# Splitting the key/value product of a streaming hybrid block into two K halves, and moving the last head's outputs

## What is computed

```
h = rmsnorm(x); p = h @ w_in            # 2816 columns, split into
qa, ka, va = 8 query heads, 2 key and 2 value heads of 64     (windowed attention)
qb, fb, ib, gb = 4 heads of 128 each                          (HGRN2 gated recurrence)
ya = attention(rope(rmsnorm(qa)), rope(rmsnorm(ka)), va)      # own 64-chunk and the one before, sinks
yb = rmsnorm(o_intra + o_inter) * silu(gb)                    # chunkwise recurrence
x = x + concat(ya, yb) @ w_out
x = x + (silu(h2 @ w_gate) * (h2 @ w_up)) @ w_down            # h2 = rmsnorm(x)
```

## Time and profile before

| what | value |
|---|---|
| median of 3 runs | 2125.22 us (2124.48 to 2125.67) |
| the profiled execution | 2124.75 us, of which 2123.0 us are the span that the trace shows |
| TensorE busy in the span | 2097.5 us (99%), 11128 matmuls |
| VectorE busy | 1305.7 us (62%) |
| ScalarE busy | 825.3 us (39%) |
| moved by transfers | 395.77 MB, mean 186 GB/s |

### The profile page before, as it was taken

How to read it: one execution, slowest core, us unless ns; L and a number is a source line. 1 busy time by engine, 2 the same in 40 slices (tenths; PEclk the granted TensorE clock), 3 DMA queues, 4 the chain that set the end, 5 groups by cost and what they waited for, 6 DMA issues and landing times.

```text
span 2123.0 us, 28527 instructions
## 1 busy us (share of the span) xinstructions
PE 2097.5 (99%) x11128; PEld 1770.7 (83%) x11128; DVE 1305.7 (62%) x1998; ACT 825.3 (39%) x1454; POOL 99.2 (5%) x108
## 2 busy tenths in 40 slices
PE   7999999999999998999999999999999999999999
PEld 7889889889988787888888888888888888888887
DVE  4674654554467875777777677777777754444332
ACT  4783573573464333433233243333333322222221
POOL 2101100100100000000000000000000000000000
PEclk9999999999999999999999999999999999999999
DMA  7857735844546675444445345545445575555532
GB/s 264 282 201 278 296 140 194 303 160 155 218 159 238 217 252 218 142 142 140 149 145 184 105 140 173 193 152 190 144 149 164 183 250 189 201 173 173 178 134 90
DMA packets 194262, 395.77 MB, mean 186 GB/s; under 512 B 11408, under 2 KB 117136, under 8 KB 172752
## 3 DMA queue, kind: packets, MB, share of 16 engines
q1 hardware_dynamic: 187616, 363.27, 49.7%
q0 software_dynamic: 6512, 30.67, 3.9%
HBM read 268.60 MB, written 125.30 MB: 186 GB/s over the span
## 4 chain that ended last, share of the span: by engine, by line
PE 60%; DVE 0%; DVEq 0%; ACT 0%; issue 0%
PE b_bank_A L373 4%; PE b_bank_A L371 4%; PE b_bank_A L372 4%; PE b_bank_C L373 4%; PE b_bank_B L373 4%; PE b_bank_C L371 4%; PE b_bank_B L371 4%; PE b_bank_B L372 4%; PE b_bank_C L372 4%; PE b_hx_bank L1985 3%; PE b_hx_bank L1984 3%; PE b_hx_bank L1986 3%; PE b_bank_D L371 2%; PE b_bank_D L373 2%; PE b_bank_D L372 2%; PE b_hx_bank L1929 1%
## 5 line engine op out<-in xcount | busy, mean ns | idle before, releaser
L1870 ACT ACTIVATE b_s_hi<-b_s_stage 128x1408 fp32r<-128x1408 f32 x56 | 77.5, 1383 | 299.9 <-PE b_hx_bank L1986 143.4
L371 PE MATMUL a_pj<-a_w_hi,a_hT_hi 128*128 128x256 f32 x640 | 185.0, 289 | 1.5 <-DVE a_hT_lo L1256 1.5
L373 PE MATMUL a_pj<-a_w_hi,a_hT_lo 128*128 128x256 f32 x640 | 180.6, 282 | 0.0
L372 PE MATMUL a_pj<-a_w_lo,a_hT_hi 128*128 128x256 f32 x640 | 180.6, 282 | 0.0
L371 PE MATMUL a_pj<-a_hT_hi,a_w_hi 128*128 128x512 f32 x384 | 154.6, 403 | 0.0
L373 PE MATMUL a_pj<-a_hT_hi,a_w_lo 128*128 128x512 f32 x384 | 150.2, 391 | 0.0
L372 PE MATMUL a_pj<-a_hT_lo,a_w_hi 128*128 128x512 f32 x384 | 150.0, 391 | 0.0
L371 PE MATMUL b_bank_A<-b_h_hi_B,b_w_hi 128*128 128x512 f32 x352 | 137.9, 392 | 0.0
L373 PE MATMUL b_bank_A<-b_h_hi_B,b_w_lo 128*128 128x512 f32 x352 | 137.4, 390 | 0.0
L372 PE MATMUL b_bank_A<-b_h_lo_B,b_w_hi 128*128 128x512 f32 x352 | 137.4, 390 | 0.0
L371 PE MATMUL b_bank_B<-b_h_hi_T,b_w_hi 128*128 128x512 f32 x352 | 137.3, 390 | 0.0
(11 more groups left out here) (309 smaller groups left out, 5080.0 us busy)
## 6 DMA issues: line engine op xcount, KB each, us to landing
b_gu_stage<-w_gu SPq DMA_DIRECT2D x44, 1024.0 KB, 5.3
b_s_stage<-a_sums SPq DMA_DIRECT2D x56, 704.0 KB, 4.1
a_w_hi<-w_parts SPq DMA_DIRECT2D x30, 1024.0 KB, 4.8
a_w_lo<-w_parts SPq DMA_DIRECT2D x30, 1024.0 KB, 7.2
a_sums<-b_a SPq DMA_DIRECT2D x88, 256.0 KB, 4.8
a_sums<-b_gate SPq DMA_DIRECT2D x66, 256.0 KB, 3.6
b_hx<-hc POOLq DMA_DIRECT2D x12, 1024.0 KB, 5.1
b_w_blocks<-w_dn SPq DMA_DIRECT2D x11, 1024.0 KB, 4.9
```

Of the source, the lines that this page charges most:

```text
L371: pe.matmul(out, stationary[0](k), moving[0](k), start=(k == 0 and not adds), stop=False, skip_group_check=adds)
L372: pe.matmul(out, stationary[0](k), moving[1](k), start=False, stop=False, skip_group_check=adds)
L373: last = pe.matmul(out, stationary[1](k), moving[0](k), start=False, stop=(k == ends), skip_group_check=adds)
L1870: act.activation(f.s_hi[n % 2][:], f.s_stage[n % 2][:], ACT.Copy).then_inc(f.s_hi_ready, 1)
```

## The change

For blocks 1 to 3 the KV chunk is no longer computed one token tile at a time. At its first group TensorE does the lower four K tiles of all four token tiles, then the upper four of tiles 0 and 1. The upper four of tiles 2 and 3 follow as groups 2 and 3, each after ScalarE has copied out the tile that shares its bank. Tiles 0 and 2 share bank 0, tiles 1 and 3 bank 1: the two results lie side by side in a bank (`kv_out`). The number of matmuls is the same. The transpose of the eighth K tile now comes after the first 12 matmuls, as before, but the product that needs it comes after 36 others.

In `LAST_HEAD`, `yt` of head 2 moves from (KV, 2) to (KV, 3), `o`, `on1` and `on2` of head 3 move from (KV, 2) to (QA0, 0), and `yt` of head 3 moves from (QA0, 0) to (QA0, 2). `ds` and `att` keep their places, (KV, 0) and (KV, 1).

```diff
-LAST_HEAD = {("KV", 0): (("on2", 2), ("ds", 3, 0), ("ds", 3, 1),), ("KV", 1): (("att", 3),), ("KV", 2): (("o", 3), ("yt", 2), ("on1", 3), ("on2", 3),), ("QA0", 0): (("yt", 3),)}
+LAST_HEAD = {("KV", 0): (("on2", 2), ("ds", 3, 0), ("ds", 3, 1),), ("KV", 1): (("att", 3),), ("KV", 3): (("yt", 2),), ("QA0", 0): (("o", 3), ("on1", 3), ("on2", 3),), ("QA0", 2): (("yt", 3),)}

+    def kv_out(b, t):
+        first = WC * (t // 2) if b > 0 else 0
+        return pj[t % 2][:, first:first + WC]
...
                     elif name == "KV":
+                        ps = kv_out(b, g)
...
-                    if (b > 0 or at >= 2) and not second_half:
+                    if b > 0 and name == "KV":
+                        if g > 1:
+                            pe.wait_ge(kv_ready.sem, kv_ready.upto(b, g - 1))
+                    elif (b > 0 or at >= 2) and not second_half:
...
-                        last = three_passes(pe, pj[at % 2][:, 0:WC], still, moving, range(KT), arrived if at == 0 else None)
-                    if kind == "proj":
+                        if name != "KV" or b == 0:
+                            last = three_passes(pe, pj[at % 2][:, 0:WC], still, moving, range(KT), arrived if at == 0 else None)
+                        else:
+                            halves = [(0, t) for t in range(TT)] + [(1, 0), (1, 1)] if g == 0 else [(1, g)] if g > 1 else []
+                            for upper, t in halves:
+                                if upper == 0 and t < 2:
+                                    pe.wait_ge(g_ready.sem, g_ready.upto(b - 1, HG - 1 + t))
+                                tokens = slice(t * P, (t + 1) * P)
+                                for k in range(upper * (KT // 2), (upper + 1) * (KT // 2)):
+                                    if t == 0:
+                                        pe.wait_ge(hT_ready.sem, hT_ready.upto(b - 1, k + 1))
+                                    starts, ends = k == 0 and t < 2, k == KT - 1
+                                    pe.matmul(kv_out(b, t), hT_hi[:, hT_slot(b, k), tokens], w_hi[s][:, k, :], start=starts, stop=False, skip_group_check=True)
+                                    pe.matmul(kv_out(b, t), hT_hi[:, hT_slot(b, k), tokens], w_lo[s][:, k, :], start=False, stop=False, skip_group_check=True)
+                                    last = pe.matmul(kv_out(b, t), hT_lo[:, hT_slot(b, k), tokens], w_hi[s][:, k, :], start=False, stop=ends, skip_group_check=True)
+                                if upper == 0 and t == 0:
+                                    next_x(b - 1, KT - 1)
+                                if upper == 1 and g == 0 and t == 0:
+                                    last.then_inc(pj_full.sem, 1)
+                    if kind == "proj" and not (b > 0 and name == "KV" and g == 1):
                         last.then_inc(pj_full.sem, 1)
```

## The result

| | before | after |
|---|---|---|
| median | 2125.00 us (7 runs, 2124.29 to 2125.67) | 2132.26 us (7 runs, 2130.31 to 2132.47) |
| the profiled execution | 2124.75 us | 2131.02 us |

The ratio is 1.0032, 95% interval 1.0023 to 1.0041. The change makes the kernel 7.3 us slower, where I had forecast +3.0 us and a range up to 2130.5.

A forecast was written before the change was run, and what follows sets the result against it. TensorE was taken as the bound, busy nearly everywhere. Two blocks losing 1.7 us each, less 0.4 kept in block 3, gave +3.0 us: 2127.75 on the profiled execution, 2128.2 us as median, range 2123.7 to 2130.5.

The forecast's parts named there:

- second weight piece: Second 1 MiB piece of output weights, loaded through SyncE's queue; forecast VectorE 3.9 us late on it in blocks 1 and 2.
- d - 2.2: Delay on VectorE less 2.2 us slack before TensorE's first query transposes; forecast 3.9 - 2.2 = 1.7 us per block.
- The stall removed: TensorE's wait for the last hT_lo in KV, blocks 1 to 3: 0.67 us each, forecast to go.
- new wait at `yt`: TensorE at yt of head 2 waits for VectorE's state update: 0.25 us per block, bounds 0 and 0.4.
- The late `yH`: SyncE's store of head 3's yH in block 1: issued at 202.5 instead of 197.45, holding weight transfers behind it.
- 3.67 MB at 385 GB/s take 9.5 us. The load lands at 214.3: SyncE's queue, block 1: weight stores and load released together after yH lands at 204.8; bounds 212.4 and 216.1.
- the slower next stretch (326 GB/s): Transfer rate used as upper bound for the queued weight transfers: 11.3 us, landing at 216.1 in block 1.
- The chain and its slack: VectorE's rotations to TensorE's first qT: nothing absorbs the delay, 2.2 us slack, 1.7 us lost in blocks 1 and 2.
- wait about 2 us at the transposes: TensorE waits about 2 us for a_qk in blocks 1 and 2, not in block 3.
- The wait at F1: ScalarE's late copy holds TensorE at the F1 group: limit of being felt, only moving part of the same wait forward.
- the second rival: Stores and load behind late yH at 326 GB/s: lands 216.1, each of two blocks loses 3.5, +6.6 us, 2131.8; chance 0.14.
- most bytes are stores: Reason given against 326 GB/s for the queued weight transfers, and for taking 385 GB/s.

The follow-up runs named there:

- e3_weights_first: The whole change, with SyncE issuing the first weight piece's stores and the second's load before waiting for yH of head 3: 2122.55 us, ratio 0.9990.
- e6_load_late_only: The kernel before, with only the load of the second weight piece moved from (QA0, 2) to (QA0, 3): 2129.14 us, ratio 1.0020.
- e9_chunk_load_waits: The whole change, with SyncE waiting for the second group of QA1 before loading the weight chunk released by QA0: 2131.17 us, ratio 1.0031.
- e8_chunk_load_held: The whole change, with the load of QA0's released chunk placed after QA1's second group but without a wait, in effect a second execution: 2131.70 us, ratio 1.0033.
- e2_moves_only: The kernel before, with only the new LAST_HEAD places and the old KV groups: 2132.61 us, ratio 1.0039.
- e7_wait_at_one_place: The whole change, with norm step qn1 of token tile 2 one group later, so ScalarE copies the last query group first: 2135.10 us, ratio 1.0050.
- e4_yt_behind_query: The whole change with weight transfers ahead of the yH wait, plus yt of head 2 moved behind the first query group: 2122.99 us, ratio 0.9991.
- e10_load_before_stores: The whole change, with the second weight piece's load issued ahead of the first piece's four stores, still behind the yH wait: 2123.16 us, ratio 0.9993.
- e1_halves_only: The whole change, with the last head's steps back at their old places, leaving the K halves alone: 2134.67 us, ratio 1.0044.

## Why the prediction was wrong

The mechanism was the forecast's, step by step. The size of one term, how long the queued transfers take, was not. The start of VectorE's work on the second weight piece, counted from the start of KV in block 1, was 34.56 us before. The delay d of that start and what the block took more:

| kernel | d | d - 2.2 | block 1 took more |
|---|---|---|---|
| `e3_weights_first` | 0.28 | hidden | -0.31 |
| `e6_load_late_only` | 4.31 | 2.1 | 2.16 |
| `e9_chunk_load_waits` | 5.36 | 3.2 | 3.21 |
| `e8_chunk_load_held` | 5.79 | 3.6 | 3.59 |
| the change | 5.82 | 3.6 | 3.64 |
| `e2_moves_only` | 6.18 | 4.0 | 3.98 |
| `e7_wait_at_one_place` | 5.78 | 3.6 | 4.92, with the low clock uncovered |

- **The stall removed.** Right. The last `hT_lo` is no longer waited for. A new wait at `yt` takes part of it. Block 3 gained 0.32 us for 0.4 forecast. `e4_yt_behind_query` shows the full 0.74 when the new wait goes too. So the stall was worth 0.74 us, not 0.67, and the wait 0.42, not 0.25: two small errors that partly cancel.
- **The late `yH`.** Right. Issued at 202.86 for 202.5. `att` directly behind `ds` takes 0.91 us, not 0.81, and the wait at `yt` was at its bound of 0.4.
- **The step that failed: "3.67 MB at 385 GB/s take 9.5 us. The load lands at 214.3".** It landed at 216.2. `yH` landed 2.4 us after its issue, at 205.3. Reckoned from there, as in the forecast, the 3.67 MB took 10.9 us, a mean of 337 GB/s. I had read the rate off a stretch that held only half of the dip (202 to 206, the dip is at 205 to 207), and had taken the slower next stretch (326 GB/s), which held the other half, for a bound only. But a dip stands beside this load in the kernel before, in the change and in `e9_chunk_load_waits`, so a rate without it was too high. The same sum (landing of `yH` at 206.7, then 1.05 MB at 385 GB/s) gives 209.4 for `e10_load_before_stores`, where the load landed at 210.9. It falls short by 1.5 us there with no store ahead of the load, and by 1.4 in the change with all four. 1.4 us of transfer, 0.4 of a later issue and 0.1 of a later landing of `yH` make 1.9 us, in two blocks 3.8, and +3.0 becomes +6.8. Of the +7.18 us read from the blocks, that leaves 0.4, most of it because block 2 lost 0.22 more than block 1, and block 3 gained 0.1 less than forecast. A mean over both stretches, 355 GB/s, would have given 10.3 us, and 2129.8 us in all.
- **The chain and its slack.** Right to 0.1 us, in the five kernels of the table with d over 4 and the low clock covered. Their second blocks agree to 0.1 us as well (the change: d of 5.98, 3.86 more). The 2.2 us of slack and the lack of anything that absorbs the delay are the table above. In the changed kernel TensorE does not wait about 2 us at the transposes, as I had forecast, because it has already lost that time at F1 and by the clock.
- **The wait at F1.** I put it "at the limit of being felt". With d = 5.8 it is 2.0 us in block 1 and 2.6 in block 2 and is the largest wait in the changed stage, apart from the start-up. It did not hold VectorE in turn: its last rotation is no later than its start on the second piece, 5.8 us. That it only moves part of the same wait forward is shown by `e7_wait_at_one_place`.
- **The chances.** This result is the second rival almost to the number: it lands at 216.1 there, with +6.6 us. I had given that 0.14 and cut the range below it. The reason against it, "most bytes are stores", was no measurement of a load behind stores. That it came so close is in part luck: it had the lower rate, and neither the later issue of `yH` nor the larger delay in block 2.

By the Trainium skill, "DMA: Bandwidth & Descriptors", section "Anatomy of one DMA", an estimate for the 3.93 MB is 11.0 us after the issue of `yH`. It took 13.3. That section gives its fit for a single transfer issued by GpSimd, and here SyncE issued six, so the forecast had stretched it. With the limit of about 358 GB/s for one core in the "Specifications" of the same Trainium skill page the estimate is 13.0 us. That is close to what was measured, but single stretches ran above that limit, at 393 and 400 GB/s in the rows above, so the agreement of the mean does not show that this limit was at work.

## What to carry to other kernels

A step that waits in an in-order queue delays every issue behind it. When such a step is moved, follow the queue to the first transfer that an engine needs, and take its slack from the trace. If that is less than the delay, issue that load before the waiting step, or at least before the stores. Price a burst of queued transfers by the mean rate of a like burst to its landing, not by its best stretch. The largest wait in the view need not be the one that costs: here removing the wait at F1 made the kernel about 3 us slower.

## What the runs showed of the hardware

- A stop of TensorE of 2.0 us (221.64 to 223.91, in an otherwise full stream) was followed about 1 us later by the lower clock for 3.4 us. The same stop in `e8_chunk_load_held` was not. The change, `e2_moves_only`, `e8_chunk_load_held` and `e9_chunk_load_waits` have eight such stops at F1 together, with 1.4 to 2.5 us of idle time in the timeline, and the clock fell behind three of them. The Trainium skill, "TensorE: Matmul & The Clock Gate", "Part 1: The HAM clock gate", states that idling halves the clock. These runs agree, but the same gap did not always do it. When nothing covers it, the low clock cost 1.3 us in block 1 of `e7_wait_at_one_place` (4.92 us more where d - 2.2 is 3.6), 2.5 us in its block 2 (6.45 where it is 3.9), and about 1.5 us in block 3 of `e1_halves_only` (3.26 more, where block 1 at the full clock took 1.71 more).
- The start of the feed-forward stage has such a low stretch too, and its length differs between executions. By stretch, 831 to 853 us, the kernel before and then `e3_weights_first`:

```profile
831.00:853.00 22.00, 19.19 (x105) 16.83 (x104) 17.25 (x18) 12.18 (x14) 3.75 (x5) 0.77 0.78 286
```

```profile
831.00:853.00 22.00, 19.79 (x120) 17.03 (x119) 19.59 (x22) 13.88 (x16) 3.85 (x6) 0.93 0.86 311
```

A mean clock of 0.77 against 0.93 over 22 us is about 10 us at half clock against 3. From the first matmul of this stage to the end the profiled execution took 1292.2 us before and 1290.0 in `e3_weights_first`. That is where the rest of its gain in the profile lies. The twelve profiled executions give no rule for it. The other ten took 1290.9 to 1291.8 us from there, the change among them with 1291.3, though it arrived 7.2 us later than the kernel before. And `e4_yt_behind_query`, with a mean clock of 0.92 in its first 22 us, took 1290.9, hardly less than `e8_chunk_load_held` with 0.79 and 1291.1. So the low stretch alone does not set the time of this stage, and a later arrival did not lengthen it. Whether the 1.2 us of `e3_weights_first` beyond the blocks are an effect of its edit or scatter stays open.
